# The second block's context rows and half of four query tiles are made during the first block's normalization, and four modulation steps move behind the value projection

## The reference

```python
x = first_block(...)                      # ends: x = x + gate * (x_mix @ w_out); rmsnorm(x, final_norm_w)
silu_c, silu_cc = silu(c_2), silu(c_ctx_2)
for l in range(2):                        # second block, two layers
    sh1, sc1, g1, sh2, sc2, g2       = split(silu_c  @ ada_w[l] + ada_b[l], 6)   # modulation, for x
    sh1c, sc1c, g1c, sh2c, sc2c, g2c = split(silu_cc @ ada_w[l] + ada_b[l], 6)   # and for the context
    h  = rms_norm(x,  norm_mix[l]) * (1 + sc1)  + sh1
    hc = rms_norm(xc, norm_mix[l]) * (1 + sc1c) + sh1c
    ...  # layer 0: q, k, v and nq, nk, nv = [h; hc] @ even_w_in, two attentions, even_w_out
    ...  # then an expert feed-forward; layer 1 likewise with other mixers
```

## Time and profile before

| | us |
|---|---|
| median of 3 runs | 1990.56 (1990.11 to 1990.93) |
| profiled execution | 1988.59 |
| its span | 1986.2 |
| PE busy | 1699.7 (86%) |
| DVE, ACT, POOL busy | 611.1, 347.2, 55.5 |
| chain that ended last | PE 42%, issue 25%, DMA 10%, DVE 4% |

### The profile page before, as it was taken

One profiled execution on the slowest core, in us unless ns is written; L12 is line 12 of the kernel. 1 busy time (PEld: TensorE's weight loads), 2 busy tenths in 40 slices (PEclk: granted clock), 3 DMA queues, 4 the chain that ended last, 5 costly groups with the idle time before them and its releaser, 6 DMA issues.

```text
span 1986.2 us, 23104 instructions
## 1 busy us (share of the span) xinstructions
PE 1699.7 (86%) x9658; PEld 857.4 (43%) x9658; DVE 611.1 (31%) x1394; ACT 347.2 (17%) x852; POOL 55.5 (3%) x51
## 2 busy tenths in 40 slices
PE   5999998898999999899999989889998766665654
PEld 3844674343444574333333323256564433232322
DVE  1157839713100773412223113140443211110101
ACT  2112226403110561100000000021441000000000
POOL 0000200010010000000000000000000000000000
PEclk9999999999999999999999999989998988788888
DMA  8241339955221103489999999921327999999996
GB/s 335 106 170 49 121 127 390 394 234 217 85 83 77 43 1 128 171 358 428 427 428 427 428 428 427 427 98 57 127 79 287 429 426 428 426 427 427 427 427 262
DMA packets 39098, 538.05 MB, mean 271 GB/s; under 512 B 4330, under 2 KB 4714, under 8 KB 6612
## 3 DMA queue, kind: packets, MB, share of 16 engines
q1 hardware_dynamic: 37860, 530.71, 64.3%
q0 software_dynamic: 1136, 5.88, 0.8%
HBM read 535.52 MB, written 1.05 MB: 270 GB/s over the span
## 4 chain that ended last, share of the span: by engine, by line
PE 42%; issue 25%; DMA 10%; DVE 4%; DVEq 1%; ACT 1%; POOL 0%; POOLq 0%; ACTq 0%
PE bank L600 40%; DMA mem<-in_moe 9%; PE bank L610 2%; DMA mem<-in_ada_w 1%; DVE mem L1342 1%; DVEq L1339 1%; DMA mem<-in_w_out 1%; POOL mem L2312 0%; DVE mem L1807 0%; DVE mem L1624 0%; ACT mem L2016 0%; ACT mem L1997 0%; DVE mem L1645 0%; DVE mem L1657 0%; DVE mem L1565 0%
## 5 line engine op out<-in xcount | busy, mean ns | idle before, releaser
L600 PE MATMUL bank<-mem 128*32 128x256 f32 (+11 forms) x8842 | 1583.1, 498 | 257.9 <-DMA mem<-in_moe 166.4
L600 PEld LDWEIGHTS bank<-mem 128*32 128x32 f32 (+4 forms) x8842 | 765.9, 148 | 1017.1 <-issue 703.0
L2016 ACT ACTIVATE mem<-bank 128x512 f32<-128x512 f32 (+5 forms) x269 | 132.6, 504 | 1067.4 <-PE bank L600 734.1
L1807 DVE TENSOR_TENSOR mem<-mem,bank 128x512 f32<-128x512 f32 (+1 forms) x32 | 17.8, 556 | 497.6 <-PE bank L600 497.6
L1824 DVE TENSOR_TENSOR mem<-bank,mem 32x512 f32<-32x512 f32 (+1 forms) x128 | 71.1, 555 | 225.3 <-PE bank L600 224.0
L610 PE MATMUL bank<-mem 128*128 128x128 f32 x760 | 121.3, 288 | 20.1 <-DVE mem L1807 4.9
L610 PEld LDWEIGHTS bank<-mem 128*128 128x128 f32 x760 | 88.3, 147 | 86.4 <-issue 45.0
L1475 DVE SCALAR_TENSOR_TENSOR mem<-mem 128x256 f32<-128x256 f32 x160 | 86.9, 543 | 10.4 <-issue 1.1
L1997 ACT ACTIVATE mem<-mem 128x1024 f32<-128x1024 f32 x22 | 23.1, 1052 | 198.1 <-DVE mem L1565 153.5
L1342 DVE TENSOR_SCALAR mem<-bank,mem 128x128 f32<-128x128 f32 (+2 forms) x136 | 45.7, 406 | 24.2 <-PE bank L610 24.2
L1971 ACT ACTIVATE mem<-bank 128x256 f32<-128x256 f32 (+2 forms) x54 | 19.7, 396 | 175.8 <-PE bank L600 175.8
(11 more groups left out here) (181 smaller groups left out, 513.2 us busy)
## 6 DMA issues: line engine op xcount, KB each, us to landing
mem<-in_moe SPq DMA_DIRECT2D x192, 2048.0 KB, 34.9
mem<-in_ada_w SPq DMA_DIRECT2D x24, 2048.0 KB, 10.8
mem<-in_w_in SPq DMA_DIRECT2D x10, 2048.0 KB, 7.8
mem<-in_w_ada SPq DMA_DIRECT2D x6, 2048.0 KB, 12.4
mem<-in_even_w_in SPq DMA_DIRECT2D x6, 2048.0 KB, 10.5
mem<-in_w_out SPq DMA_DIRECT2D x4, 2048.0 KB, 9.1
mem<-in_odd_w_in SPq DMA_DIRECT2D x3, 2048.0 KB, 19.8
mem<-in_even_w_out SPq DMA_DIRECT2D x2, 2048.0 KB, 7.6
```

What stands on the lines that cost most here:

```text
L600: return nc.tensor.matmul(o, lhsT, rhs, start=start, stop=stop, skip_group_check=True)
L2016: took(name, S.activation(o, i, func))
```

## The change

Five edits belong together.

1. The chunk order. ada2.8 to ada2.11 now stand behind even2. The list reads w_out0 to w_out3, even0, even1, even2, ada2.8 to ada2.11, even3 and so on, with the same modulo-3 slots.
2. The context alone. POOL loads `ctx_2` once the tile y11 is done, before `group_rstd(3)`. ACT squares the two context tiles, POOL takes the new root `norm2c`, ACT scales the rows. PE transposes them in the new `ctx_T`, between w_out2 and w_out3, and DVE and ACT modulate the tiles nTc.0 to nTc.7 into `hT`'s context columns.
3. q0 to q3. Their context columns (256 to 511) are made right behind the first block's projection, before `norm_T(2)`; their x columns behind it. The four PSUM tiles stay open between.
4. `norm_T(2)` handles two tiles of x rows instead of four: 16 transposes instead of 32.
5. Steps 26 to 29 are issued behind v3, `ada_cols(2)` and the gates behind nq. On POOL the load and the masking of `na_bias` come before the router's load.

```diff
         for i in range(4):
             chunk(f"w_out{i}", "w_out", i, D)
-            if i == 1:
-                chunk("ada2.8", "ada_w1", 8, 512)
-        for i in range(21, 24):
-            chunk(f"ada{i // 12 + 1}.{i % 12}", f"ada_w{i // 12}", i % 12, 512)
         for i in range(6):
             chunk(f"even{i}", "even_w_in", i, 512)
+            if i == 2:
+                for k in range(20, 24):
+                    chunk(f"ada{k // 12 + 1}.{k % 12}", f"ada_w{k // 12}", k % 12, 512)
...
-        NORM_TILES = [4, 2, 4, 4, 4, 2, 2]
+        NORM_TILES = [4, 2, 2, 4, 4, 2, 2]
...
+            def ctx_T():
+                pe.wait_ge(ctx_xn, 2)
+                for kt in range(KT):
+                    t = B.open(f"nTc.{kt}", "act" if kt % 2 else "dve")
+                    for j in range(2):
+                        last = tr(t.ps[:, P * j:P * j + P], xn[:, 2 + j, P * kt:P * kt + P])
+                    B.close(t, last)
...
+                    if i == 2:
+                        ctx_T()
                     if i == 1:
-                        ada_rows(26)
                         for k in (10, 11, 16, 17):
                             ada_gate(k)
                         group_rows(3)
...
             project_block1()
-            for k in range(27, 30):
-                ada_rows(k)
+            w = use("even0")
+            wait_took(pe, "nTc.6")
+            wait_took(pe, "nTc.7")
+            q_open = [B.open(f"q{m}", "act") for m in range(4)]
+            for m in range(4):
+                feature_major(q_open[m], w, P * m, P, SEQ, TOK, o=q_open[m].ps[:, SEQ:TOK])
             norm_T(2)
...
+                if i < 4:
+                    B.close(q_open[m], feature_major(q_open[m], w, P * m, P, 0, SEQ))
...
             done_with("even2")
-            ada_cols(2)
-            for k in (22, 23, 28, 29):
-                ada_gate(k)
+            for k in range(26, 30):
+                ada_rows(k)
...
+                if i == 3:
+                    ada_cols(2)
+                    for k in (22, 23, 28, 29):
+                        ada_gate(k)
...
+            dve.wait_ge(ctx_sums, 2)
+            scaled(meansq[:, 2:4], ssq[:, 2:4], 1.0 / D, EPS, ALU.mult, ALU.add).then_inc(ms_done, 1)
             for k in (10, 11, 16, 17):
                 ada_gate(k)
             group_out(3)
+            settle()
+            for kt in range(0, KT, 2):
+                ctx_modulate(kt)
...
+            act.wait_ge(ctx2_in, 16)
+            for j in range(2, 4):
+                S.activation(xn[:, j, :], xres[:, j, :], ACT.Square, accum_out=ssq[:, j:j + 1]).then_inc(ctx_sums, 1)
+            act.wait_ge(rstd_done, POW.index("norm2c") + 1)
+            for j in range(2, 4):
+                S.activation(xn[:, j, :], xres[:, j, :], ACT.Identity, scale=rstd[:, j:j + 1]).then_inc(ctx_xn, 1)
...
+            pool.wait_ge(mm_done, tiles["y11"].no)
+            pool.dma_start(xres[:, 2:4, :], A["ctx_2"][0].rearrange("(t p) d -> p t d", p=P)).then_inc(ctx2_in, 16)
             group_rstd(3)
+            roots("norm2c", rstd[:, 2:4], meansq[:, 2:4])
             pool.dma_start(gain_1, A["final_norm_w"].unsqueeze(0).to_broadcast([P, D])).then_inc(arena_in["gain1"], 16)
-            pool.dma_start(xres[:, 2:4, :], A["ctx_2"][0].rearrange("(t p) d -> p t d", p=P)).then_inc(ctx2_in, 16)
```

More of the change, by code:

```diff
@@ L563, in build @@
         router_pad = sem("router_pad")
+        ctx_sums, ctx_xn = sem("ctx_sums"), sem("ctx_xn")
         d_squared = sem("d_squared")
@@ L566, in build @@
         part_used, ada_used = sem("part_used"), sem("ada_used")
-        POW = ["norm0", *(f"norm1.{j}" for j in range(2)), "norm2", "diff_a", "diff_b", *(f"norm3.{j}" for j in range(4)), "norm4", "lat", "ret",
+        POW = ["norm0", "norm2c", *(f"norm1.{j}" for j in range(2)), "norm2", "diff_a", "diff_b", *(f"norm3.{j}" for j in range(4)), "norm4", "lat", "ret",
                *(f"norm5.{j}" for j in range(2)), "norm6"]
@@ L943, in _ @@
             for i, (name, m) in enumerate(QK):
[L944 to L947, removed]
+                if i == 4:
+                    w = use("even1")
+                if i < 4:
+                    B.close(q_open[m], feature_major(q_open[m], w, P * m, P, 0, SEQ))
+                else:
+                    t = B.open(f"{name}{m}", "act")
+                    B.close(t, feature_major(t, w, P * m, P, 0, TOK))
                 if m == 3:
@@ L1399, in modulate, with ctx_modulate @@
                 took(name, last)
+            def ctx_modulate(kt):
+                ps = arrive(dve, f"nTc.{kt}")
+                took(f"nTc.{kt}", scaled(hT[:, kt, SEQ:TOK], ps[:, 0:SEQ], norm_a[:, NORM_A[2], 2 * kt + 1:2 * kt + 2], ada_col[1][:, 0, 2 * kt + 1:2 * kt + 2], ALU.mult, ALU.add))
             def norm_T(n):
@@ L1984, in squares @@
             def squares(n, done=None, before=0, sums_of=None):
-                for j in (2, 3, 0, 1) if n == 2 else range(NORM_TILES[n]):
-                    if n == 2 and j < 2:
+                for j in range(NORM_TILES[n]):
+                    if n == 2:
                         act.wait_ge(xn_done, NORM_SUM[0] + j + 1)
@@ L2120, in _ @@
             pair_squares(11)
+            act.wait_ge(ctx2_in, 16)
[4 more added lines that the diff above has]
+                S.activation(xn[:, j, :], xres[:, j, :], ACT.Identity, scale=rstd[:, j:j + 1]).then_inc(ctx_xn, 1)
+            for kt in range(1, KT, 2):
+                ps = arrive(act, f"nTc.{kt}")
+                took(f"nTc.{kt}", S.activation(hT[:, kt, SEQ:TOK], ps[:, 0:SEQ], ACT.Identity,
+                                               scale=norm_a[:, NORM_A[2], 2 * kt + 1:2 * kt + 2], bias=ada_col[1][:, 0, 2 * kt + 1:2 * kt + 2]))
             squares(1, res_done)
-            act.wait_ge(ctx2_in, 16)
             squares(2)
-            other_rows(2)
-            act.wait_ge(mm_done, tiles["col17"].no)
-            take("ag2", ada_row, arrive(act, "ag2")[:, :])
             norm_T(2)
@@ L2144, in _ @@
                 take(f"v{j}", v_tok[:, j, :], arrive(act, f"v{j}")[:, :])
+            act.wait_ge(mm_done, tiles["col17"].no)
+            take("ag2", ada_row, arrive(act, "ag2")[:, :])
             for m in range(4):
@@ L2356, in _ @@
             norm_roots(2)
[L2357 to L2360, removed]
             pool.wait_ge(mm_done, tiles["nT2.7"].no)
@@ L2365, in _ @@
             Q.tensor_tensor(nb, nb, C("na_mask").unsqueeze(1).to_broadcast([P, 48, GRID_W]), ALU.add).then_inc(na_masked, 1)
+            pool.wait_ge(mm_done, tiles["col29"].no)
+            Q.memset(router_sb, 0.0).then_inc(router_pad, 1)
+            pool.wait_ge(router_pad, 1)
+            load_router(0)
             roots("diff_a", d_ss[:, 0:12], d_ms[:, 0:12])
```

## The result

The changed kernel takes 2000.93 us (median of 5 runs, 1998.18 to 2001.57) against 1990.11 us (5 runs, 1986.21 to 1990.93). The ratio is 1.0054 with a 95% interval of 1.0040 to 1.0069: slower by 10.7 us, where +5.4 us was forecast and the range ended at +8.9 (1999.5). Each ratio in this document is one of mean times, so it can differ a little from the quotient of two medians. The profiled execution took 2001.41 us with a span of 1999.5.

What follows compares the result with a forecast made beforehand. PE was taken to bound the kernel, busy in 86% of the span. Terms -6.4 + 9.5 + 0.8 + 1.5 = +5.4 us on the median before of 1990.56 gave 1996.0 us, range 1992.0 to 1999.5.

Steps and rivals of the forecast that it cites:

- Term 1: Behind the first block: waits and low clock of 7.5 us vanish, 1.1 us of new waits remain; -6.4 us.
- Term 2: Behind v3: three chunk loads queue ahead of nq while PE has only four short steps; +9.5 us idle.
- Term 3: At nq: PE's clock may be low after the waits; +0.8 us, bounds 0 and 1.7.
- Term 4: Ahead of w_out0: the earlier ctx_2 load takes bandwidth and delays w_out0 and PE; +1.5 us, bounds 0 and 2.4.
- B: Rival, large ends: ctx_2 wholly ahead of w_out0, nq starts at 1.2 GHz; +7.2 us, 1997.8 us; chance 0.15.
- A: Rival, small ends: ctx_2 costs nothing and the clock stays up at nq; +3.1 us, 1993.7 us; chance 0.17.
- C: Rival, faster: the three loads behind v3 come in time; -4.9 us, 1985.7 us; chance 0.06.
- D: Rival: x rows' normalization not hidden behind q's context products; at most 0.5 to 1 us, no chance of its own.

Runs made afterwards that it cites:

- q tiles one by one: Changed kernel with each q tile opened just ahead of its own context products instead of all four at once: 1995.35 us, ratio 1.0036 to the kernel before.
- filled wait at w_out0: Changed kernel with 4 products of the identity, which nothing reads, issued in PE's wait for w_out0: 1998.12 us in one run.

## Why the prediction was wrong

The direction and the main mechanism, the waits behind v3, were right; the size was half. The sum of +5.4 us stands against +11.8 in the stretch and +10.7 in the runs. The four terms were off by 2.5, 0.2, 0.9 and 2.3 us, all in one direction.

**Term 1, -6.4 us: it measured -3.9 us.** All that was to vanish did vanish. The x rows' normalization was hidden: DVE had them at 475.83, and PE came to their transposition at 482.12.

```profile
474.41 1.42 DVE L1409 TENSOR_SCALAR mem<-mem 128x1024 f32<-128x1024 f32 x2 [0.83 <-POOL mem L2346]
```

What was to stay was under-priced by 2.5 us: 5.1 us were booked for the two transpositions with their waits and for opening q3, and 2.61 + 1.41 + 3.47 = 7.5 us were taken, with 0.2 us in the split products. Two steps failed. The larger is "Opening q3 waits for DVE to take the second row's first sum, under 0.1 us". q3 gets the bank of the second row's second sum, the very last. DVE had to take the first sum, add it to x and take the second before that bank was free, and PE stood for 1.41 us. This is shown by opening the tiles one by one. The other is "its 8 tiles share the 4 banks that the open sums leave". The tile `ag2` is open from step 18 to step 29, so it holds a fifth bank throughout, and only three are left. Read from the program's PE list with bank numbers, w_out3's last sums and what follows:

```
L600 MATMUL bank3<-mem 128x512
L600 MATMUL bank0<-mem 128x256 x8
L600 MATMUL bank1<-mem 128x256 x8
L600 MATMUL bank2<-mem 128x256 x8
L600 MATMUL bank3<-mem 128x256 x8
L610 MATMUL bank4<-mem 128x128 x2
L610 MATMUL bank5<-mem 128x128 x2
L610 MATMUL bank7<-mem 128x128 x2
```

The q tiles take exactly the banks of the four sums. `ctx_T` and `norm_T(2)` go round three banks, 4, 5 and 7, while 6 is `ag2`'s; the waits of 0.20 us stand there. `ctx_T` took 0.3 us and `norm_T(2)` 0.7 us more than booked. That this is due to the third bank is read from the order and was not tried.

**Term 2, +9.5 us: right.** nq began at 575.93, 17.9 us behind v3's end at 558.06, where 17.5 was forecast, and even3 landed 14.2 us after its issue at 561.66. PE's waits are 4.53 + 1.59 + 2.14, and 1.4 us of low clock in step 28 are hidden in them: 9.7 us. Spreading the steps took the waits away.

**Term 3, +0.8 us: the clock at nq measured 1.7 us.** The term took the middle of its bounds, and the upper one came. In the six traces with these three waits unfilled nq took 87.74 us in four and 86.04 us in two (q tiles one by one, filled wait at w_out0); in those two PE was at 1.2 GHz through most of steps 28 and 29 and had it behind it when nq began. The rule that the prediction took from the Trainium skill's "TensorE: Matmul & The Clock Gate" (section "Part 1: The HAM clock gate"), throttled by default and released by activity, led it to the upper bound, which came in both traces of the changed kernel and not in those two variants.

**Term 4, +1.5 us: it measured 3.8 us.** The step that failed is "So what `ctx_2` takes of the bandwidth delays w_out0 and PE one to one". The delay itself was 0.63 us at step 25 and 1.47 us at w_out0, 2.1 us, within its bounds. But the longer wait also took PE's clock down behind it, 1.7 us more. I had priced that effect behind v3 and not here, though the argument is the same. The early load alone on the kernel before shows the whole term, +3.5 us.

The bytes fit the delay. The first packets of `ctx_2` moved at 394 us, 4 us after the load was issued at 390.13; the 0.3 us that the prediction took off for a start-up stood on no row. From 394.5 to 402.3 us the queues were shared like this (queue, packets, MB, share of the 16 engines; q1 is SP's, q0 POOL's):

```profile
q1 hardware_dynamic: 176, 2.61, 78.6%
q0 software_dynamic: 175, 0.72, 22.6%
```

0.72 MB at the 426 GB/s of that window is 1.7 us. The packets are equal in number and not in size: POOL's hold 4 KB, most of SP's 16 KB. The prediction read in the Trainium skill's "DMA: Bandwidth & Descriptors" (section "Queues, rings and completion order") that an engine takes turns packet by packet, and the trace agrees, 176 to 175. Its step from there, "An equal turn would bring nearly all of `ctx_2` in ahead of w_out0", took equal turns for equal bytes; they gave POOL's queue 22% of the bytes.

Together: -3.9 + 9.7 + 1.7 + 3.8 = +11.3 of the +11.8 us in the stretch; 0.5 us remain without a cause. That the runs give 10.7 and not 11.8 us is within their interval.

The rivals: B, the large ends, was nearest with +7.2 us, or +8.9 with the second low stretch that it names without a place; that stretch came, behind w_out0. It was still short, by the 2.5 us of term 1, for which no rival had a place. A and C did not occur, nor did D. The range was too narrow because the bounds of term 1 allowed for under 0.5 of these 2.5 us, and because the clock, 0.9 + 1.7 us, had an upper end at one place only.

## What to carry to other kernels

Short steps that each need a whole weight chunk should be spread among long ones: in a ring of three slots, four of them in a row cost 9.7 us of waiting, and spread they cost no wait and 1.1 us more of PE's time. A wait of PE of some us can have a second price, 1.4 to 1.7 us in these traces for the clock behind it. It can be met by filling the wait, and it falls away if another wait behind it hides it. When tiles are kept open over other work, list which bank each one gets and who must empty it first, with every tile that is open, however old, and ask for each bank as late as possible. When two DMA queues share the engines, compare the sizes of their packets before pricing what one takes from the other.

## What the runs showed of the hardware that was not expected

POOL's masking of `na_bias` moved beside the rotation of q on DVE. POOL's and DVE's rows in the changed kernel:

```profile
491.91 5.62 POOL L2397 TENSOR_TENSOR mem<-mem 128x3072 f32<-128x3072 f32 x1 [6.15 <-DMA mem<-in_na_bias]
```
```profile
493.30 0.43 DVE L1616 TENSOR_TENSOR mem<-bank,mem 128x256 f32<-128x256 f32 x1 [8.05 <-PE bank L600]
493.64 4.17 DVE L1617 TENSOR_TENSOR mem<-mem 128x256 f32<-128x256 f32 x1
...
499.17 0.42 DVE L1617 TENSOR_TENSOR mem<-mem 128x256 f32<-128x256 f32 x1
```

The same DVE instruction takes 0.42 us a moment later. Here it took 4.17 us and ended at 497.81 us, just after POOL's at 497.53; in the eight other traces with this order it took 4.22 to 4.69 us. The DVE instruction just ahead of it, which reads one of its two inputs from a PSUM bank, took its usual 0.43 us while POOL's was running (the row at 493.30). The Trainium skill's "SBUF — State Buffer" (section "Who interferes with whom") says that DVE and GpSimd share a pair of ports with an exclusive lock, and that a DVE instruction with two inputs in SBUF contends with a GpSimd instruction that reads SBUF; the traces agree with both (SBUF is `mem` in the rows). In the five traces of the kernel before and its variants, where the masking runs later, every such instruction of the rotation took 0.42 or 0.43 us. ACT's take of q2 came late by it, but PE had no wait, so it cost nothing here.

Whether a wait brings the low clock is not told by its length alone: ahead of w_out0, 3.5 us brought it in all six traces where nothing filled them; 2.07 us did in one trace (33.61 us for 80 records) and did not in five others.

Two queues that shared the DMA engines from 394.5 to 402.3 us took turns by packet, 176 to 175, and not by bytes, 2.61 to 0.72 MB.
